# Sixty-four bytes of padding behind one SBUF tile of a two-block transformer kernel

## The reference

```python
    hx = rmsnorm(x, g_pre) * (1 + scale[:, None]) + shift[:, None]
    q, k, v, ga, uf, gf, zc, bc, cc, gc = split_cols(hx @ w_in, PROJ_SIZES)
    a = window_attention(q, k, v, kc, vc, sink_b)
    f = fourier_mix(uf, w_fourier)
    s = short_conv_mix(zc, bc, cc, conv_w, conv_b)
    y = gated_merge(a, ga, f, gf, s, gc, w_out)
    x_new = x + gate[:, None] * rmsnorm(y, g_post)
```

```python
        mx = (s_lat @ ada_w[l] + ada_b[l]).reshape(bsz, N_MOD, 1, d)
        x = x + 0.5 * mx[:, 2] * swiglu(ada_norm(x, norm_g[l, 0], mx[:, 0], mx[:, 1]), ffn_w_in[l, 0], ffn_w_out[l, 0])
        # even layer: differential attention + mLSTM; odd layer: gated linear attention
        x = x + mx[:, 5] * yx
        x = x + 0.5 * mx[:, 8] * swiglu(ada_norm(x, norm_g[l, 2], mx[:, 6], mx[:, 7]), ffn_w_in[l, 1], ffn_w_out[l, 1])
    return rms_norm(x, final_g)
```

## Time and profile before

| | us |
|---|---|
| timed runs, median of 3 | 2313.49 |
| lowest and highest | 2308.47, 2314.11 |
| profiled execution, span from first to last instruction | 2314.2 |
| TensorE busy in it | 2227.1 (96%) |
| weight loads (beside the matmuls) | 2091.2 (90%) |
| VectorE busy | 1145.4 (49%) |
| ScalarE busy | 846.8 (37%) |
| GpSimd busy | 176.3 (8%) |

### The profile page before, as it was taken

The page is one execution under the profiler, slowest core; times in us unless marked ns, Lnnn a source line. Parts: engine busy times, 40 slices in busy tenths (PEclk is TensorE's granted clock), DMA queues, the critical chain, the costliest instruction groups (busy, mean ns, idle before and its releaser), DMA issues. The chain is left out here.

```text
span 2314.2 us, 46991 instructions
## 1 busy us (share of the span) xinstructions
PE 2227.1 (96%) x19320; PEld 2091.2 (90%) x19320; DVE 1145.4 (49%) x1930; ACT 846.8 (37%) x1384; POOL 176.3 (8%) x150
## 2 busy tenths in 40 slices
PE   6999999899999999998999999999999999999998
PEld 5986798799999999976999999999999998979998
DVE  5227375653433445456653333454343446487665
ACT  4226454632221233248432222243232234455444
POOL 0003112100000010501200000010000010001000
PEclk9999999999999999999999999999999999999999
DMA  9853544445676244520354666242233233225573
GB/s 297 234 167 86 172 133 104 128 147 154 186 216 186 86 131 117 149 80 28 102 175 141 190 207 189 84 126 85 81 114 94 86 96 101 74 82 146 168 202 112
DMA packets 515900, 315.76 MB, mean 136 GB/s; under 512 B 16035, under 2 KB 513274, under 8 KB 515622
## 3 DMA queue, kind: packets, MB, share of 16 engines
q1 hardware_dynamic: 515160, 313.45, 46.1%
q10 hardware_dynamic: 590, 0.16, 0.0%
HBM read 312.50 MB, written 1.06 MB: 135 GB/s over the span
## 5 line engine op out<-in xcount | busy, mean ns | idle before, releaser
L1118 PE MATMUL ps<-h_hi,w_hi 128*128 128x256 f32 x3376 | 728.0, 280 | 3.5 <-DVE h_lo L1726 1.7
L1118 PE MATMUL ps<-h_lo,w_hi 128*128 128x256 f32 x3376 | 720.6, 278 | 0.0
L1118 PE MATMUL ps<-h_hi,w_lo 128*128 128x256 f32 x3376 | 720.6, 278 | 0.0
L1118 PEld LDWEIGHTS ps<-h_hi,w_hi 128*128 128x128 f32 x3376 | 537.8, 189 | 22.9 <-issue 21.6
L1118 PEld LDWEIGHTS ps<-h_lo,w_hi 128*128 128x128 f32 x3376 | 539.4, 189 | 0.1
L1118 PEld LDWEIGHTS ps<-h_hi,w_lo 128*128 128x128 f32 x3376 | 537.9, 189 | 0.0
L1960 DVE TENSOR_TENSOR w_lo<-stage,w_hi 128x1024 fp32r<-128x1024 f32 x227 | 285.0, 1258 | 441.5 <-ACT w_hi L1467 440.9
L1467 ACT ACTIVATE w_hi<-stage 128x1024 fp32r<-128x1024 f32 x227 | 236.6, 1055 | 334.4 <-PE ps L1118 200.4
L1960 DVE TENSOR_TENSOR w_lo<-deep,w_hi 128x1024 fp32r<-128x1024 f32 x184 | 226.1, 1234 | 226.9 <-ACT w_hi L1467 225.2
L1467 ACT ACTIVATE w_hi<-deep 128x1024 fp32r<-128x1024 f32 x184 | 191.9, 1055 | 179.7 <-PE ps L1118 141.4
L1118 PE MATMUL ps<-g_hi,w_hi 128*128 128x256 f32 x1100 | 232.9, 280 | 0.2
(11 more groups left out here) (413 smaller groups left out, 2858.0 us busy)
## 6 DMA issues: line engine op xcount, KB each, us to landing
modw<-in_ada_w SPq DMA_DIRECT2D x72, 1024.0 KB, 6.7
stage<-in_ffn_w_in SPq DMA_DIRECT2D x88, 512.0 KB, 3.9
deep<-in_ffn_w_in SPq DMA_DIRECT2D x88, 512.0 KB, 3.9
modw<-in_w_mod SPq DMA_DIRECT2D x18, 1024.0 KB, 6.1
stage<-in_w_in SPq DMA_DIRECT2D x30, 512.0 KB, 5.3
stage<-in_ffn_w_out SPq DMA_DIRECT2D x32, 384.0 KB, 3.5
stage<-in_even_w_in SPq DMA_DIRECT2D x24, 512.0 KB, 4.0
deep<-in_ffn_w_out SPq DMA_DIRECT2D x32, 384.0 KB, 3.4
```

Source lines behind the costliest of these rows:

```text
L1118: last = mm(ps[:, j, v - a:v - a + SEQ], w_part[wp][:, u % RING, c, :], x_part[xp][:, x, v:v + SEQ], start=first and wp == xp and v == a, ...
```

## The change

16 more fp32 values, 64 bytes per partition, are reserved behind the token-major tile:

```diff
@@ -357,7 +357,7 @@
-        sizes = {"resid": KC * NT, "big": 24 * NT, "hT": KC * NT, "mixT": KC * NT, "vtok": TT * D + TT * ML_HEADS, "stage": STAGE * KC * P,
+        sizes = {"resid": KC * NT, "big": 24 * NT, "hT": KC * NT, "mixT": KC * NT, "vtok": TT * D + 2 * TT * ML_HEADS, "stage": STAGE * KC * P,
                  "scr": 2 * RING * KC * P, "modw": 2 * KC * SEG,
                  "wfbd": 4 * P, "svec": 2 * KC * 34}
```

## The result

The changed kernel takes a median of 2373.36 us (4 runs, 2372.65 to 2377.49), against 2313.01 us for the kernel before beside it (4 runs). The ratio is 1.0268, with a 95% interval of 1.0254 to 1.0283: 2.7% slower, some 60 us. The forecast was no change, and its range ended at 2321 us.

A forecast was written before the change was run, and what follows sets the result against it. TensorE, busy 2227.1 of 2314.2 us, was taken as the bound; splits, operands, paces and transfers each counted 0, and less 0.7 gave 2313.5 us, taken as 2313.0. Its own range was 2306 to 2320 us, for 8 in 10 2304 to 2321.

The forecast's parts named there:

- Weight load and moving operand of TensorE: TensorE's operand reads: equal fp32 matmul medians of 379 ns taken to show no static cost of the 64 bytes; 0 us.
- The two paces: Main-line matmuls follow at 113.4 or 117.6 ns, not chosen by addresses alone; redraw has mean 0, spread +-5 us.
- Rival 2: Main-line matmuls slow as operands on one boundary collide: 10.3 us (2323.8 us), at the extreme 40 us; chance 0.05.
- Rival 1: The 64 bytes make stretches slow; 13 slow main-line stretches become fast, 16.3 us gained, 2297 us; chance 0.07.
- ScalarE and VectorE splits: Copies and subtractions that split weights: alignment hardly matters; cost 0, bounds -1.7 and +0.3 us.
- Transfers: DMA into staging tiles: felt only in the first 58 us; value 0, bound 1.2 us, by the skill's rule 2 us.
- Rival 3: Redraw of main-line paces goes far one way, net 1650 matmuls: 7 to 9 us either way; chance 0.10.

The follow-up runs named there:

- e11: Small kernel, TensorE streams only: eight operand distances for fp32r with 256 columns, fp32 with 256 and fp32r with 512; 647.5 us.
- e10: Small kernel, TensorE streams only: distances 52, 64, 76, 180, 192 and 204 at five token addresses, four passes; 760.17 us.
- e3: Kernel before with the whole stretch of tiles starting 64 bytes later, distances between weight slots and token tiles kept; 2313.64 us, ratio 0.9994.
- e7: Kernel before with only scr (weight slots) moved up by 192 bytes, giving distance 0 to h; 2390.72 us, ratio 1.0334.
- e2: Kernel before with staging, modulation and small tiles at the changed kernel's remainders by 256, weight slots left in place; 2311.42 us, ratio 0.9991.
- e9: e8 plus staging tiles and modw on a multiple of 256 bytes, as in the changed kernel; 2304.88 us, ratio 0.9949 against the kernel before.
- e1: Kernel before with only scr (weight slots) moved up by 64 bytes, the other tiles keeping their remainders by 256; 2373.48 us, ratio 1.0252.
- e6: Kernel before with only scr (weight slots) moved up by 128 bytes, giving distance 192 to h; 2355.93 us, ratio 1.0175.
- e8: Kernel before with w_hi and w_lo 12 bytes later inside scr, giving distance 76 in place of 64; 2303.93 us, ratio 0.9938.
- e4: Small kernel, TensorE only: 45 streams of 96 fp32r matmuls of 128x256, each at another pair of weight and token addresses; 555.65 us.

## Why the prediction was wrong

**The step that failed** is "Weight load and moving operand of TensorE", with its conclusion that "a static cost of the 64 bytes is not there. Taken value 0". It rested on lines 945 and 2939, with operands on the same and on different multiples and 379 ns for both the earlier trace rows. They are plain fp32, and in e11 fp32 has 215.8 ns at all eight distances. The main line is fp32r, and its own comparison, 276 against 280 ns between lines 1118 and 1162, was put aside as the two paces. It pointed the right way, though one row couldn't show it: line 1162 is distance 192, where in e10 18 of 20 streams ran at 117 ns or more, and the main line is distance 64, where 16 of 20 ran at 113.3. The term taken as 0 measured 55.8 us in the table above. From the spacings of before it comes out as 9,838 of 112 to 115 ns x (118.7 - 113.4) = 52, and 5,919 of 116 to 120 ns x (118.7 - 117.8) = 5, together 57.

**"The two paces"** described the trace rightly and drew too much from it. That the same tiles run at 113.4 and at 117.6 ns shows that the addresses don't choose alone. It doesn't show that they have no say, and I took the two values as the only ones there are. Distance decides which set of paces a stream can have; at 64 there are two, at 128 only 118.4 to 118.9 ns was seen, slower than both. e3 is what the forecast would have been right for.

**Rival 2** was the right mechanism ("operands on one boundary collide", "where the 64 bytes kept them apart"), in the right place, with a chance of 0.05. Its price of 10.3 us for one stretch and 40 us for the extreme was too low on two counts: it counted only line 1118's 13,428 matmuls of some 15,600, and it priced them by the step to the known second pace, 4.2 ns, where the new distance costs 5.3 (and 0.9 for the matmuls that were slow already). Nor is "one boundary" the whole of it: absolute multiples mean nothing (e3), and at distance 128 operands are not at the same place by 256, only by 128. Distance 0, which is, costs more still (e7).

**Rival 1** had the effect the wrong way round. Its evidence, 389 ns with wgate_hi and 396 with wlr_hi, fits e11: wgate_hi is at distance 0 from h, wlr_hi at 64, and with 512 columns distance 0 is the best, with 256 columns the worst. The rows were sound and could not be carried to the other shape. After the change wlr_hi is at 128, and the median of its matmuls with h_hi is 392 instead of 396, but with h_lo it went up, from 394 to 398; wgate_hi's stayed at 389. For wlr_hi, which loads 64 columns, no run gives the rule:

```profile
L2482 PE MATMUL ps<-h_hi,wlr_hi x8: 392/392/392, 2002.7 to 2007.6; 128*64 128x512 f32 x8
```

**ScalarE and VectorE splits** held: a change of 5 ns on an engine that waits, and the weight queue's wait for w_lo in line 1118 (total us, times, longest) is 1.3 us where the earlier trace rows had 1.7.

```profile
PEld ps L1118 <- DVE w_lo L1960: 1.3, 3, 0.4
```

**Transfers** held in sign and size. Queue time per packet, share x 16 engines x span / 515,160, is 33.1 ns before and 31.9 after, over packets of all sizes. All kernels with staging on a multiple of 256 have 31.9 to 32.0 (e2, e3, e9), all others 33.1 to 33.2 (e1, e6, e7, e8), for instance e2:

```profile
q1 hardware_dynamic: 515160, 313.45, 44.6%
```

That is 3.7%, and e2's 0.9991 (0.9973 to 1.0008) is its worth for the time: nothing measurable. The 397,607 packets of 512 bytes alone took a mean of 29.0 ns before and 28.3 after, the 99,632 of 1024 bytes 50.6 and 47.3. The rule of the Trainium skill, "DMA: Bandwidth & Descriptors", section "How a descriptor splits into AXI transactions", has the right direction, but if a packet of 512 bytes cost by its beats (22 to 16), it would cost 27% less; measured were 2% less. The measurement decides: the price of these packets doesn't follow the beats. On the matmuls, the Trainium skill's page "TensorE: Matmul & The Clock Gate", section "Step-by-step: what each phase is for", says that TensorE has two independent ports for reading SBUF and that loading the next tile's weights takes no read bandwidth from the running matmul. With fp32r of 256 columns the runs don't fit a load that is free at every address: the spacing goes from 113.3 to 120.0 ns with nothing but the distance changed (e4). That the two reads meet in the memory is the likely reading; no run looks into it.

**Rival 3**, the redraw of the paces, exists as described: e2 and e3 mixed them anew and stayed within 0.3% of before.

What stays open: how the memory is built that gives this dependence with a period of 256 bytes and its fine structure (113.3 ns at 52, 64 and 76, but not at 68 and 72); what chooses the pace when a stream begins; and why the granted clock fell more often in e8.

## What to carry to other kernels

Where TensorE is busy nearly all the time and loads new weights for every matmul of 256 columns, the distance between loaded and streamed operand is a setting worth a sweep: a stream of 48 matmuls per distance in a small kernel tells it, and it predicted whole-kernel times to 4 us for the bad distances, and was 14 us off for the good one (e8). Repeat each distance several times, since some have more than one pace. Read the pace from starts or from counts in a window; the duration of a record tells only the fastest pace from the rest. Never judge it by matmuls of another type or width. A tile moved to a rounder address is a change to every pair of tiles in which it takes part.

## What the runs showed of the hardware that was not expected

- The spacing of 128x256 fp32r matmuls with a weight load each depends on the address of the loaded operand less that of the streamed one, by 256 bytes: 113.3 or 117.8 ns at 64, 117.8 or 113.3 at 192, 118.7 at 128, 120.0 at 0; up to 123.7 among steps of 4 bytes.
- At distance 64, 52 and 192 a stream may come out at either of two paces and keeps it; both occur in a small kernel where only TensorE works during a stream (e10).
- fp32 matmuls (215.8 ns a pass) don't depend on it at the eight distances tried; fp32r ones with 512 columns do, with 0 as the best (226.7 ns against 233).
- Packets into staging rows on a multiple of 256 bytes take 31.9 to 32.0 ns of queue time each, against 33.1 to 33.2 at 192 past one; the 512-byte ones alone 28.3 against 29.0 to 29.2.
